# Single-pass products in latent attention, GpSimd-spread row sums, a shorter prefix sum

## The reference

```python
def parallel_mixer(h, w_in, ..., w_q_b, w_kv_b, out_norm_gqa, out_norm_mla, w_o, ...):
    proj = h @ w_in
    q_g, k_g, v_g, q_lat, kv_lat = jnp.split(proj, IN_OFFSETS, axis=-1)
    ...
    c_q = rms_norm(q_lat, mla_q_norm)                     # (512, 256)
    q_m = (c_q @ w_q_b).reshape(B, S, MLA_HEADS, MLA_QK_DIM)      # 8 heads of 64 + 32
    q_m = jnp.concatenate([q_m[..., :64], apply_rope(q_m[..., 64:], cos_m, sin_m)], axis=-1)
    c_kv = rms_norm(kv_lat[..., :MLA_KV_RANK], mla_kv_norm)       # (512, 128)
    k_rope = apply_rope(kv_lat[..., MLA_KV_RANK:]...)             # 32 columns, one for all heads
    kv = (c_kv @ w_kv_b).reshape(B, S, MLA_HEADS, 64 + 64)
    k_m = jnp.concatenate([kv[..., :64], broadcast(k_rope)], axis=-1)
    v_m = kv[..., 64:]
    o_m = blocked_attention(q_m[:, :, :, None, :], k_m, v_m, MLA_QK_DIM ** -0.5)
    merged = jnp.concatenate([rms_norm(o_g, out_norm_gqa), rms_norm(o_m, out_norm_mla)], axis=-1)
    return merged @ w_o

def expert_choice_moe(h, w_router, w_gate, w_up, w_down):
    affinity = jax.nn.softmax(h @ w_router, axis=-1)
    gate, idx = lax.top_k(jnp.swapaxes(affinity, 1, 2), cap)     # 64 of 512 tokens for each of 16 experts
    ...
```

## Time and profile before

| | |
|---|---|
| runs, median (lowest to highest) | 3004.63 us (3003.12 to 3005.75) |
| profiled execution, from first to last instruction | 3003.8 us |
| mean granted TensorE clock | 0.977 |
| TensorE busy | 2816.4 us, 94% |
| VectorE busy | 1422.1 us, 47% |
| ScalarE busy | 1129.1 us, 38% |
| GpSimd busy | 238.4 us, 8% |

### The profile page before, as it was taken

The page is one execution under the profiler, slowest core; times in us unless marked ns, Lnnn a source line. Parts: engine busy times, 40 slices in busy tenths (PEclk is TensorE's granted clock), DMA queues, the critical chain, the costliest instruction groups (busy, mean ns, idle before and its releaser), DMA issues.

```text
span 3003.8 us, 40104 instructions
## 1 busy us (share of the span) xinstructions
PE 2816.4 (94%) x16212; PEld 2094.2 (70%) x16212; DVE 1422.1 (47%) x2150; ACT 1129.1 (38%) x1920; POOL 238.4 (8%) x229
## 2 busy tenths in 40 slices
PE   7999979989999979999999789999999999799998
PEld 5657854536658745447877578888888787578886
DVE  6665532237666333244555763333334654753444
ACT  4664431124665321135233652222222542643332
POOL 0011020000011110001011010000001111000001
...
GB/s 157 29 43 59 86 173 415 415 366 64 29 29 100 100 237 418 414 395 127 144 115 153 40 76 113 112 114 128 124 84 16 88 122 130 81 84 99 98 99 28
DMA packets 67909, 428.28 MB, mean 143 GB/s; under 512 B 7968, under 2 KB 8352, under 8 KB 20368
## 3 DMA queue, kind: packets, MB, share of 16 engines
...
## 4 chain that ended last, share of the span: by engine, by line
PE 82%; DVE 7%; DMA 4%; ACT 4%; issue 2%; POOL 2%; SPq 0%; DVEq 0%; ACTq 0%; POOLq 0%
PE banks L854 78%; PE banks L855 4%; DMA weight<-in_w_up 3%; ACT arena L1685 3%; DVE arena L2390 3%; POOL arena L3200 2%; DVE arena L3046 1%; DVE arena L2679 0%; DVE weight_part L2494 0%; DMA block_tokens_high<-df_stage 0%; DVE arena L2677 0%; DMA weight<-in_ada_w 0%; ACT weight_part L1685 0%; DVE x L2390 0%; POOL block_tokens_low L3214 0%
## 5 line engine op out<-in xcount | busy, mean ns | idle before, releaser
L1685 ACT ACTIVATE arena<-banks 128x512 f32<-128x512 f32 (+2 forms) x513 | 281.2, 550 | 885.0 <-PE banks L854 779.4
L854 PE MATMUL banks<-weight,arena 128*64 128x512 f32 (+4 forms) x2136 | 429.1, 573 | 21.3 <-DMA weight<-in_w_up 9.2
L854 PE MATMUL banks<-hidden,weight_part 128*128 128x512 f32 (+1 forms) x2304 | 446.8, 355 | 0.0
L854 PEld LDWEIGHTS banks<-hidden,weight_part 128*128 128x128 f32 x2304 | 381.2, 189 | 70.4 <-issue 3.8
L854 PE MATMUL banks<-tokens_high,weight_part 128*128 128x512 f32 (+1 forms) x1536 | 409.0, 357 | 10.0 <-ACT tokens_high L1685 10.0
L2494 DVE TENSOR_TENSOR weight_part<-weight,weight_part 128x2048 fp32r<-128x2048 f32 x124 | 285.8, 2308 | 194.8 <-ACT weight_part L1685 194.7
L1685 ACT ACTIVATE weight_part<-weight 128x2048 fp32r<-128x2048 f32 x124 | 236.4, 1908 | 349.7 <-PE banks L854 336.4
L854 PEld LDWEIGHTS banks<-weight,arena 128*64 128x64 f32 (+2 forms) x2136 | 150.9, 135 | 255.4 <-issue 233.8
L854 PEld LDWEIGHTS banks<-tokens_high,weight_part 128*128 128x128 f32 x1536 | 273.9, 190 | 62.5 <-DVE arena L2390 16.0
L3200 POOL TENSOR_TENSOR arena<-arena 128x512 f32<-128x512 f32 (+1 forms) x89 | 116.0, 1303 | 1974.3 <-ACT arena L1685 1707.4
L854 PE MATMUL banks<-tokens_low,weight_part 128*128 128x512 f32 (+1 forms) x768 | 264.7, 354 | 0.0
...
## 6 DMA issues: line engine op xcount, KB each, us to landing
weight<-in_w_gate SPq DMA_DIRECT2D x64, 1024.0 KB, 13.6
weight<-in_w_up SPq DMA_DIRECT2D x64, 1024.0 KB, 8.1
weight<-in_w_down SPq DMA_DIRECT2D x64, 1024.0 KB, 11.2
weight<-in_w_ff SPq DMA_DIRECT2D x64, 1024.0 KB, 4.8
weight<-in_ada_w SPq DMA_DIRECT2D x48, 1024.0 KB, 6.3
weight<-in_w_in SPq DMA_DIRECT2D x28, 1024.0 KB, 5.2
weight<-in_w_o SPq DMA_DIRECT2D x8, 1024.0 KB, 4.8
weight<-in_w_mem_kv SPq DMA_DIRECT2D x8, 1024.0 KB, 4.9
```

The source lines that it names most:

```text
L854: mm = lambda o, a, b, first=True, last=True: eng.matmul(o, a, b, start=first, stop=last, skip_group_check=True)
L1685: act = lambda o, i, f=ACT.Copy, **k: eng.activation(o, i, f, **k)
```

## The change

**Latent attention in split parts.** `w_q_b` and `w_kv_b` get high and low parts in weight slots; the normed latents get them too (`latent_q_high` and so on), as do the queries and keys of each head (`mla_high_a` and so on, `mla_low`). Head projections, value projections and latent scores go by `tile3`. For each prepared head ScalarE now writes the keys' high part straight from the bank and rounds the key rope (heads 0 to 5; the last two take over buffers in which it still stands), and rounds the rotated queries two steps after the preparation (`mla_high`). VectorE takes the keys' low part from the bank, one step after the preparation, behind the rope instructions, and it is this subtraction that now frees the bank; for heads 0 to 3 it takes the rope's low part, and two steps after the preparation the queries' (`mla_low`). The split of `w_kv_b` stands where the one of `w_o`'s first piece did; the split of `w_q_b` is in step 2, the latents' parts are made in step 3; `w_o` is split in steps 6, 28, 30 on ScalarE and one step later on VectorE.

**Row sums.** For pairs of heads GpSimd's new `spread` copies the 8 columns of reciprocals into 512 columns, 64 times each, and `shares` transposes the four 128 x 128 blocks of that. Memory attention, with one head at a time, transposes the broadcast column without the spread. The load of the memory tokens stands behind the last `spread` and waits for the last latent score.

**Router.** The prefix sum becomes one product with "before" over all 64 columns and three with "one" over the 48, 32 and 16 columns to the right of each block.

The diff, cut to its core:

```diff
+    tiles = lambda name, at, n: Carve(at * T).rounded(f"{name}{l}", n, T)
+    b.update(CQL=tiles("latent_q_low", 23, 2), CKVL=tiles("latent_kv_low", 25, 1)[:, 0, :], CQH=tiles("latent_q_high", 39, 2), CKVH=tiles("latent_kv_high", 41, 1)[:, 0, :])
...
+    pairs_of = lambda a: [(a[:, 2 * i, :], a[:, 2 * i + 1, :]) for i in range(2)]
+    highs = pairs_of(first) + pairs_of(second) + [tuple(last[0:2]), tuple(last[2:4])] + pairs_of(second)
...
-        eng.wait_ge(*after(("rs", okey)))
+        eng.wait_ge(*after(("rs" if heads == 1 else "spread", okey)))
         o = take_bank(("rb", okey))
-        r = S["RS"].get(okey)
-        rows = P // heads
         for q in range(nq):
-            for h in range(heads):
-                i = mm(o[rows * h:rows * h + rows, q * P:(q + 1) * P], r[:, q * heads + h:q * heads + h + 1].broadcast_to([P, rows]), mat("ident"))
-        i.then_inc(*done(("out", ("rb", okey)), S["RS"].free(okey)))
+            i = tr(o[:, q * P:(q + 1) * P], S["RS"].get(okey)[:, q:q + 1].broadcast_to([P, P]) if heads == 1 else S["RB"].get(okey)[:, q * P:(q + 1) * P])
+        i.then_inc(*done(("out", ("rb", okey)), *((S["RS"].free(okey),) if heads == 1 else ())))
     def attend_blocks(pus, S, score, V, blocks, okey, nq, between=None, turn_lag=1, value_lag=2, late=False):
...
-                wcur[:] = [weight(("w_q_b", l)), wcur[1]]
+                wcur[:] = [weight_parts(("w_q_b", l)), wcur[1]]
             wq, wkv = wcur
-            eng.wait_ge(*after(("cqn", l)))
-            tile(("qm", l, h), [wq[:, k, P * h:P * h + P] for k in range(2)], [S["CQ"][:, k, :] for k in range(2)],
-                 free=(WF(("w_q_b", l)),) if h == HQ - 1 else ())
-            eng.wait_ge(*after(("ckvn", l)))
-            tile(("km", l, h), [wkv[:, P * h:P * h + NOPE]], [S["CKV"]], rows=NOPE,
-                 free=(WF(("w_kv_b", l)),) if h == HQ - 1 else ())
+            eng.wait_ge(*after(("cql", l)))
+            tile3(("qm", l, h), halves(wq, h, range(2)), [(S["CQH"][:, k, :], S["CQL"][:, k, :]) for k in range(2)],
+                  free=(WF(("w_q_b", l)),) if h == HQ - 1 else ())
+            eng.wait_ge(*after(("ckvl", l)))
+            tile3(("km", l, h), [tuple(a[:, P * h:P * h + NOPE] for a in wkv)], [(S["CKVH"], S["CKVL"])], rows=NOPE,
...
         def mla_score(pu):
             _, _, j, q = pu
             for u in heads_of(pu):
                 h = 2 * j + u[4]
-                eng.wait_ge(*after(("qmr", l, h)))
-                tile(("S", u), [S["QM"].get((l, h))[0:QK, q * P:q * P + P]], [S["KM"].get((l, h))[0:QK, :]],
-                     free=(S["QM"].free((l, h)), S["KM"].free((l, h))) if q == TB - 1 else ())
+                eng.wait_ge(*after(("kml", l, h)))
+                eng.wait_ge(*after(("qml", l, h)))
+                tile3(("S", u), [tuple(a[h][0:QK, q * P:q * P + P] for a in (S["QMH"], S["QML"]))], [tuple(a[h][0:QK, :] for a in (S["KMH"], S["KML"]))],
+                      free=(S["QM"].free((l, h)), S["KM"].free((l, h))) if q == TB - 1 else ())
...
+                    wcur.append(weight_parts(("w_kv_b", l)))
                 wkv = wcur[1]
-                tile(("vm", l, c), [S["CKV"][:, c * P:c * P + P]], [wkv.rearrange("p (h x) -> p h x", x=P)[:, :, NOPE:P]])
+                tile3(("vm", l, c), [tuple(S[n][:, c * P:c * P + P] for n in ("CKVH", "CKVL"))],
+                      [tuple(a.rearrange("p (h x) -> p h x", x=P)[:, :, NOPE:P] for a in wkv)])
...
-        for c in range(TB):
-            for b in range(c + 1):
-                i = mm(o[:, c * EXPERTS:(c + 1) * EXPERTS], mat("before" if b == c else "one"), S["MK"][:, b, :], b == 0, b == c)
+        mm(o[:, 0:TB * EXPERTS], mat("before"), S["MK"].rearrange("p c e -> p (c e)"), True, False)
+        for b in range(TB - 1):
+            later = TB - 1 - b
+            i = mm(o[:, (b + 1) * EXPERTS:TB * EXPERTS].rearrange("p (c e) -> p c e", c=later), mat("one"),
+                   S["MK"][:, b:b + 1, :].broadcast_to([P, later, EXPERTS]), False, b == TB - 2)
...
-            m = S["KM"].take((l, h))
+            S["KM"].take((l, h))
             if S["KM"].former:
                 eng.wait_ge(*after(S["KM"].former))
-            copy(m[0:NOPE, :], ("km", l, h), PB.get(("km", l, h))[0:NOPE, :])
-            eng.wait_ge(*after(("ks", l)))
-            act(m[64:96, :], S["KR"][64:96, :]).then_inc(*done(("kmr", l, h)))
-            eng.wait_ge(scalar_step, done.count)
+            if h == 0:
+                eng.wait_ge(*after(("ks", l)))
+            if h == 2:
+                eng.wait_ge(*after(("out", ("S", ("g", l, 3, TB - 1, 1)))))
+            if h == 4:
+                eng.wait_ge(*after(("out", ("og", l, 3))))
+            eng.wait_ge(*after(("out", ("km", l, h))))
+            act(S["KMH"][h][0:NOPE, :], PB.get(("km", l, h))[0:NOPE, :]).then_inc(*done(("kmh", l, h)))
+            if h < 6:
+                act(S["KMH"][h][64:96, :], S["KR"][64:96, :]).then_inc(*done(("krh", l, h)))
+        def mla_high(h):
+            eng.wait_ge(*after(("qmr", l, h)))
+            act(S["QMH"][h][0:QK, :], S["QM"].get((l, h))[0:QK, :]).then_inc(*done(("qmh", l, h)))
...
+                split_high(("w_q_b", l))
+            if i == 3:
+                eng.wait_ge(*after(("low", l, 4)))
+                round_tiles([S["CKVH"]], [S["CKV"]], lambda k: ("ckvn", l), lambda k: ("ckvh", l))
+                round_tiles([S["CQH"][:, j, :] for j in range(2)], [S["CQ"][:, j, :] for j in range(2)], lambda j: ("cqn", l), lambda j: ("cqh", l, j))
+            if i - 2 in PREP_AT:
+                mla_high(PREP_AT.index(i - 2))
...
-            if i in (6, 10):
-                split_high(("w_o", l, (i - 2) // 4))
+            if i in (6, 28, 30):
+                split_high(("w_o", l, (6, 28, 30).index(i)))
...
-        split_low(("w_o", l, 0))
+        split_low(("w_kv_b", l))
...
             tt(q[R, :], q[R, :], S["TBB"][R, :], ADD).then_inc(*done(("qmr", l, h)))
-            eng.wait_ge(vector_step, done.count)
+            eng.wait_ge(*after(("kmh", l, h)))
+            low, key = S["KML"][h], ("km", l, h)
+            tt(low[0:NOPE, :], PB.get(key)[0:NOPE, :], S["KMH"][h][0:NOPE, :], SUB).then_inc(*done(PB.free(key), *((("kml", l, h),) if h >= 4 else ())))
+            if h < 4:
+                eng.wait_ge(*after(("krh", l, h)))
+                tt(low[R, :], K[R, :], S["KMH"][h][R, :], SUB).then_inc(*done(("kml", l, h)))
+        def mla_low(h):
+            eng.wait_ge(*after(("qmh", l, h)))
+            tt(S["QML"][h][0:QK, :], S["QM"].get((l, h))[0:QK, :], S["QMH"][h][0:QK, :], SUB).then_inc(*done(("qml", l, h)))
...
+                split_low(("w_q_b", l))
+            if i == 3:
+                low_tiles([S["CKVL"]], [S["CKV"]], [S["CKVH"]], lambda k: ("ckvh", l), lambda k: ("ckvl", l))
+                low_tiles([S["CQL"][:, j, :] for j in range(2)], [S["CQ"][:, j, :] for j in range(2)], [S["CQH"][:, j, :] for j in range(2)],
+                          lambda j: ("cqh", l, j), lambda j: (("cql", l),) if j else ())
...
                 mla_rope(PREP_AT.index(i - 1))
+            if i - 2 in PREP_AT:
...
+    def spread(okey, S, nq):
+        b = S["RB"].take(okey)
+        if S["RB"].former:
+            eng.wait_ge(*after(S["RB"].former))
+        eng.wait_ge(*after(("rs", okey)))
+        eng.tensor_copy(b[:, 0:nq * P].rearrange("p (a b) -> p a b", a=2 * nq),
+                        S["RS"].get(okey)[:, 0:2 * nq].unsqueeze(2).broadcast_to([P, 2 * nq, P // 2])).then_inc(*done(("spread", okey), S["RS"].free(okey)))
...
+            spread(("og", l, j), S, TB)
         for h in range(HQ):
             q = S["QM"].get((l, h))[64:96, :]
             eng.wait_ge(*after(("qr", l, h)))
             eng.tensor_tensor(q, q, S["TAB"][64:96, 2, :], MUL).then_inc(*done(("qc", l, h)))
             eng.wait_ge(pool_step, done.count)
-            if h == 2:
-
-                eng.wait_ge(*after(("out", ("S", ("g", l, 3, TB - 1, 1)))))
-                eng.dma_start(B["mem", l]["MR"], A["mem"].rearrange("(k p) t -> p k t", p=P)).then_inc(small[("mem", l)], 16)
+            if h in (0, 2):
+                spread(("og", l, 2 + h // 2), S, TB)
+            if h in (4, 6):
+                spread(("om", l, h // 2 - 2), S, TB)
             if h == 4:
                 add_squares(S, [(("og", l), T)])
+        for j in range(2, 4):
+            spread(("om", l, j), S, TB)
+        eng.wait_ge(*after(("out", ("S", ("m", l, 3, TB - 1, 1)))))
+        eng.dma_start(B["mem", l]["MR"], A["mem"].rearrange("(k p) t -> p k t", p=P)).then_inc(small[("mem", l)], 16)
```

43 lines of the change are left out of this document (30 added, 13 removed).

## The result

| | before | changed |
|---|---|---|
| runs, median (lowest to highest), us | 3005.19 (3003.12 to 3006.87) | 3035.26 (3033.49 to 3038.67) |
| profiled execution, first to last instruction, us | 3003.8 | 3031.7 |
| mean granted TensorE clock | 0.977 | 0.970 |
| TensorE, VectorE, ScalarE, GpSimd busy, us | 2816.4, 1422.1, 1129.1, 238.4 | 2794.3, 1461.0, 1142.1, 257.8 |

The changed kernel is slower: the ratio is 1.0103, with a 95% interval of 1.0088 to 1.0117, some 30 us. The forecast was 3009 us with a range to 3025. TensorE has 22 us less to do, as a whole, and the program takes 28 us longer, so time must have gone into waits.

A forecast was written before the change was run, and what follows sets the result against it. TensorE was taken to bound the first attention. Per layer, -14.8 (products and shares) + 17.1 (bank wait) + 5.3 (entry) - 5.5 (elsewhere) = +2.1 us, +4 for two: 3009 us, 8-in-10 range 2981 to 3025.

The forecast's parts named there:

- The bound: Latent half of the first attention: TensorE busy for all of 32.00 us, so edits there pay or cost directly.
- (a): Head preparation: eight times three full-precision products become nine single-pass ones, 2.91 to 2.04 us each time; -7.0 us a layer.
- (b): Latent scores: 16 latent steps go from 3.82 to 3.62 us; -3.2 us a layer.
- (c): The four value projections: 0.97 to 0.68 us each; -1.2 us a layer.
- (d): Eight share steps of the latent attention: eight products become four transposes, 0.87 to 0.44 us; -3.4 us a layer.
- (e): Steps 13 to 28: TensorE's scores wait for VectorE's later subtraction to free the keys' bank; +17.1 us a layer.
- rival B: VectorE becomes the bound of the latent half, its rope instructions also slowed by GpSimd: 3024 us, chance 0.21.
- (f): Attention entry, steps 2 to 4: query-weight split and latent roundings delay maxima, first stop 2.6 us; +5.3 us a layer.
- (g): GpSimd's spread copies and the later memory-token load stay hidden under other work: 0 us.
- (h): Outside the attention: router -2.7, memory attention's shares -1.7, neighbourhood attention's -1.1, differential attention 0; together -5.5 us a layer.
- Rival A: Latent attention: the bank wait doesn't bind, shrinking to some 3 us a layer; 2981 us, chance 0.24.
- collision term: Six preparing steps: VectorE's rope instructions lose 0.6 us each while GpSimd adds squares, ahead of the bank's release.

The follow-up runs named there:

- keys_early: The changed kernel with VectorE's bank-freeing subtraction for the keys' low part moved one step ahead: 2993.49 us, ratio to before 0.9959.
- shares_only: The kernel before with only the row sums spread by GpSimd and turned by TensorE: 2992.70 us, ratio to before 0.9952.

## Why the prediction was wrong

- **The bound, right.** TensorE's stream set the time of the attention, and any stop in it is paid in full.
- **Terms (a) and (b), right, and low.** From the transposes of step 11 to those of step 12, with a preparation between them, keys_early takes 5.21 us and before 6.08: 0.87 a head, as forecast. A latent step without one takes 3.49 against 3.82: 0.33 instead of 0.2, since the six products of two latent scores follow each other at 0.23 (160.12 to 161.51 in the changed kernel, 1.39 us), without the 0.2 of edge that had been charged. (b) is 5.3 us a layer rather than 3.2.
- **Term (c), half right.** In steps 5 to 7 a value projection takes 0.97, 0.87 and 0.89 us against 1.06 before: 0.1 to 0.2 each instead of 0.3, some 0.6 a layer instead of 1.2. The three terms together are 12.9 us a layer, between the 11.4 of the rows and the 14.6 that was worked out from the Trainium skill, page FP8 and Floating Point Precision, section TensorE Precision Notes; in the preparation one product saved 0.29 us, where a quarter of 0.97 is 0.24.
- **Term (d), right.** In shares_only the attention takes 3.6 us less, for 3.4; the whole gives 13.0 where the terms of both blocks sum to 12.4.
- **Term (e), the bank wait, right in its mechanism and a little low in size**: 21.0 us a layer for 17.1. Half of what was missed is step 21, where the rope instructions collide with GpSimd's squares. The prediction had that row and put it into rival B only. The rest is 0.7 in step 25, where VectorE also waits 1.36 us for the queries' high part ahead of the norm (208.62), and 1.1 in step 27, whose reason is not shown.
- **The step that failed: the sum took a stop for its own length.** It priced 17.1 us of silence on TensorE at 17.1 us, with every product behind it at the durations of a trace in which the clock stood at 1.00. In the changed kernel the products behind four of the eight stops of layer 0 and six of the eight of layer 1 run at half clock, for a loss of 10.1 and 11.0 us. The window of the earlier trace rows with a clock of 0.74, in a stretch where TensorE pauses often, was in the rows and was read only for its busy times. A smaller piece was left out as well: a stop in a latent step costs more than the idle time shown. In the changed kernel the step from 161.51 to 166.42 is 3.73 us without its stop of 1.18, and the one from 172.37 to 177.72 is 3.72 without its 1.63, where keys_early takes 3.49; for the grouped ones it is 0.07 each. That makes an estimate of 1.6 us a layer.
- **The sum again.** Stops longer by 3.9, 10.6 of clock in the mean and 1.6 of edges are 16 us a layer above the forecast; (b), (c), (d) and (f) are 3 below it, and the rest of the program is 3.6 below it in all, 1.1 of that ahead of the first attention. With them the forecast's difference of 4 becomes 27 us, where 28 were measured between the two profiled executions.
- **Term (f), the entry, right in its first stop, and in its sum partly by luck**: 4.2 us for 5.3. The stop of step 3 is 2.67 for 2.6. The second came to 1.32 us in layer 1; in layer 0 1.7 us of half clock, which the term didn't have, stood in its place.
- **Terms (g) and (h).** The spreads cost 0, right. The router gives 2.6 a layer (2.7 forecast). Behind the attentions the difference falls by 13.5 us in all, of which 11 were forecast. The second block's part, 5.7 us, was put at 2.2; 5.4 of it appear in the second block's first layer, ahead of its feed-forward part, and shares_only has 3.7 in the whole second block. The granted clock in that block differs from kernel to kernel, and how much of the gain is the shares' and how much the clock's stays open.
- **Rival A** assumed the mechanism away. keys_early is the kernel in which the bank doesn't bind, and it took 2993, not 2981, since waits stood behind the waits. **Rival B** had the right side and the wrong reason: 3024 from VectorE's load, which at 69% in the stretch was no bound; only its collision term was real, once, in one step. The condition that it named, 90% busy, failed.
